# Ticks that end with the query products, and routing placed in the next pass's norm and first recurrence steps

## The chip, the cores and the metric

The kernel runs on one core of one Trainium2 chip. The core has five engines that run their own instruction streams and meet at semaphores: TensorE (PE, matrix products into PSUM; PEld is its weight load), VectorE (DVE), ScalarE (ACT), GpSimd (POOL) and SyncE (SP). Here POOL and SP do no arithmetic: they issue transfers, which all share the core's 16 DMA engines. The metric is the device time of one execution in microseconds (us), lower is better.

## What is computed

A two-layer encoder trunk is applied to two sequences of 256 tokens with 1024 features, in float32. Each layer adds a mixer (a bidirectional state-space recurrence with 8 groups, a dilated attention, a gated merge) and then a feed-forward step whose experts are picked per token:

```python
q = (xt @ w_query).reshape(T, PEER_HEADS, 2, PEER_HALF)
s = jnp.einsum('thsk,snk->thsn', q, sub_keys)
sv, si = lax.top_k(s, PEER_TOPK)                      # 16 of 128, twice per head
cand = sv[:, :, 0, :, None] + sv[:, :, 1, None, :]
cv, ci = lax.top_k(cand, PEER_TOPK)                   # 16 pairs per head
idx = i1 * PEER_N_KEYS + i2
g = jax.nn.softmax(cv, axis=-1)
...
hid = gelu(einsum('td,thkd->thk', xb, expert_u[ib]))
out = einsum('thk,thkd->td', gb * hid, expert_v[ib])
```

With 8 heads and 16 picks a token has 128 expert rows. A row of `expert_u` and the same row of `expert_v` lie side by side in memory, 8 KB together.

## The kernel before

**Passes.** There are four passes (two layers, two sequences each); pass m works on sequence m % 2. A pass has a mixer and 256 ticks. The mixer of pass m runs through the phases `norm`, `ssd` (8 groups), `att` (4 head pairs), `mrg` (8 columns), `out`, `norm2`, `query` (16 products, and after each second one the key scores of a head) and `route`. Its weights come in units of 512 KB, issued by SP into a ring of six slots (L447).

**Ticks.** A tick of pass p is one expert slot for 128 tokens. POOL gathers 128 expert rows of 8 KB, 1 MB in all (L518). DVE multiplies the u half with the normed input and sums it to `hid` (L1374). ACT makes gelu, the weight `wgt` and, where PE is to add the row up, a diagonal matrix `diag` (L993, L997, L1004). Three ticks later the v half is added up, by PE into the PSUM tile `sums` (L810) or by DVE into `x` (L1383); a percentage for each phase says how many of the sums are PE's. There are 8 row buffers `rows`. POOL issues the gather of tick k + 4 at the place of tick k, and that gather first waits for the sum of tick k - 4. When a half is done DVE adds `sums` to `x` (`add_sums`, L1364).

**The order of work.** The ticks of pass m - 1 run during the mixer of pass m. Each engine's program is written out by `together`: the mixer is a generator that yields a place on a planned time line (`EACH` and `TIMES`, the planned us of a phase), and ticks are put in as soon as their due time `DUE` is at or before that place. `TICKS` says how many ticks fall due in each phase and which percentage of sums is PE's. ACT takes each tick 3 planned us late (`BEHIND`). The plan sets the order alone; the engines wait for semaphores. Pass 3's ticks follow after the last mixer with nothing beside them.

**Routing.** `route(m, t, piece)` on DVE turns key scores of 128-token tile t into row numbers in 21 pieces. Pieces 0 to 7 take the best 16 of each head's two score lists, and run in the query phase, both tiles after each other, as soon as ACT has copied that head's scores (`q_sv`). Pieces 8 to 20 are the "late" ones: 8 adds up the candidates, 9 to 12 pick 16 of 112 for two heads each, 13 to 19 turn positions into key numbers, 20 writes `idx` (L1113) and releases the gathers through `i_ok`. `gates` is the softmax's last part, with an Exp on ACT (`softmax`, L832) ahead of it. For tile 0 the late pieces stand in the phase `route` at the end of the pass; for tile 1 they stand in the next pass's first two groups (`LATE_PIECES`).

**Norm.** In `norm` ACT squares x, DVE scales it (L1141), PE transposes it (L563) and DVE writes `hT` (L1147). Then PE makes the step sizes dt (L576), DVE and ACT turn them into decays in a chain of small steps (L1162 to L1181), and PE sums those (`decay_sums`, which waits for `dt_a`). Passes 2 and 3 may square x only once all ticks of the pass two before have been added.

## Time and profile before

| | us |
|---|---|
| median of 3 runs (4110.14 to 4112.36) | 4110.7 |
| the profiled execution, its own time | 4107.11 |
| its span, first to last instruction | 4105.3 |
| PE busy | 3515.4 (86%) |
| DVE busy | 2855.3 (70%) |
| ACT busy | 1838.1 (45%) |
| POOL busy | 1235.4 (30%) |
| moved by DMA | 1444.53 MB, mean 352 GB/s |
| chain that ended last | PE 29%, DMA 29%, DVE 21%, ACT 13%, issue 7% |

The span is the time from the first to the last instruction; a stretch of it is read with the view that gives, for any window, the busy time of each engine, TensorE's granted clock and what the DMA engines moved. The passes can be found in it by the writes of `idx`, which start at 667.0, 1591.9, 2520.3 and 3449.1 us for tile 0.

### The profile page before, as it was taken

To read this page: it belongs to the slowest core of one execution; us is meant where nothing else is said; L and a number is where in the kernel's file an instruction comes from. 1 tells how busy PE (TensorE), PEld (TensorE's weight loads), DVE (VectorE), ACT (ScalarE), POOL (GpSimd) and SP (SyncE) were. 2 spreads that over 40 slices of the span, in tenths; PEclk is the share of its full clock that TensorE was granted. 3 is DMA by queue.
4 is the path that set the end of the run, shared out by engine and by line. 5 is a ranking of instruction groups with operands and counts; after the bars stand their busy time and mean duration, and the time that the engine had idled before them with its cause. 6 is when DMAs were issued, how large, how long until landed. Compare 5 with 4: busy or idle time off the path is not lost.

```text
span 4105.3 us, 41298 instructions
## 1 busy us (share of the span) xinstructions
PE 3515.4 (86%) x13534; PEld 2377.2 (58%) x13534; DVE 2855.3 (70%) x5587; ACT 1838.1 (45%) x4774; POOL 1235.4 (30%) x1094
## 2 busy tenths in 40 slices
PE   7999995998889786989889886989889787778787
PEld 6877874666667564666667664666667663222222
DVE  3631137899877778899877768899787778655454
ACT  4643012676435323676435323676544422343333
POOL 1000001333433322334333322333443223433332
PEclk9999997999999998999999898999999998999999
DMA  6543445999999986999999986999999986999998
GB/s 206 180 153 129 149 136 197 374 418 424 419 412 424 423 336 247 365 423 421 425 416 424 422 335 249 355 424 415 420 423 424 423 341 250 426 427 427 427 427 359
DMA packets 252123, 1444.53 MB, mean 352 GB/s; under 512 B 31608, under 2 KB 31608, under 8 KB 118788
## 3 DMA queue, kind: packets, MB, share of 16 engines
q0 software_dynamic: 164976, 1133.94, 67.4%
q1 hardware_dynamic: 86800, 307.82, 20.2%
q8 instruction: 108, 1.77, 0.2%
q14 instruction: 107, 0.88, 0.1%
q10 hardware_dynamic: 132, 0.12, 0.0%
HBM read 1439.31 MB, written 7.13 MB: 352 GB/s over the span
## 4 chain that ended last, share of the span: by engine, by line
PE 29%; DMA 29%; DVE 21%; ACT 13%; issue 7%; POOL 1%; DVEq 0%; ACTq 0%; POOLq 0%
DMA rows<-in_w_uv,idx 28%; PE banks L551 15%; DVE rows L1374 5%; PE sums L810 5%; DVE x L1383 4%; ACT arena L871 4%; PE banks L766 3%; DVE arena L1191 3%; PE banks L810 2%; ACT diag L1004 1%; ACT L871 1%; ACT L993 1%; PE banks L717 1%; DVE arena L1290 1%; PE banks L687 1%
## 5 line engine op out<-in xcount | busy, mean ns | idle before, releaser
L518 POOL DMA_INDIRECT rows<-in_w_uv,idx x1024 | 1188.0, 1160 | 2198.1 <-DVE x L1383 1114.4
L1374 DVE CUSTOM_DVE_ANT_0 rows<-rows,xn 128x1024 f32<-128x1024 f32 x1024 | 1244.1, 1223 | 568.6 <-DMA rows<-in_w_uv,idx 564.9
L551 PE MATMUL banks<-hT,ring 128*128 128x256 f32 x6656 | 1505.2, 384 | 56.2 <-ACT arena L916 51.5
L551 PEld LDWEIGHTS banks<-hT,ring 128*128 128x128 f32 x6656 | 1277.4, 193 | 320.5 <-issue 85.5
L810 PE MATMUL sums<-rows,diag 128*128 128x512 f32 x1772 | 885.4, 630 | 193.6 <-ACT diag L1004 174.3
L993 ACT ACTIVATE gelu<-hid 128x1 f32<-128x1 f32 x1024 | 205.6, 201 | 1312.4 <-DVE hid L1374 1308.2
L810 PEld LDWEIGHTS sums<-rows,diag 128*128 128x128 f32 x1772 | 333.2, 199 | 600.3 <-ACT diag L1004 302.6
L1383 DVE SCALAR_TENSOR_TENSOR x<-rows,wgt,x 128x1024 f32<-128x1024 f32 x453 | 580.8, 1282 | 0.0
L1191 DVE SCALAR_TENSOR_TENSOR arena<-banks,pr,arena 128x254 f32<-128x254 f32 (+1 forms) x512 | 245.6, 482 | 128.7 <-ACT arena L897 115.0
L997 ACT ACTIVATE wgt<-gelu,gate 128x1 f32<-128x1 f32 x1024 | 302.6, 295 | 33.5
L810 PE MATMUL banks<-rows,diag 128*128 128x512 f32 x512 | 253.9, 618 | 62.0 <-ACT diag L1004 62.0
L1004 ACT ACTIVATE diag<-cst,wgt 128x128 f32<-128x128 f32 x571 | 229.8, 402 | 18.6
L871 ACT ACTIVATE arena<-arena 128x128 f32<-128x128 f32 x768 | 231.6, 393 | 9.4 <-DVE arena L1205 8.8
L551 PE MATMUL banks<-yT,ring 128*128 128x256 f32 x1024 | 226.7, 379 | 0.0
L810 PEld LDWEIGHTS banks<-rows,diag 128*128 128x128 f32 x512 | 86.7, 189 | 229.2 <-ACT diag L1004 167.9
L551 PEld LDWEIGHTS banks<-yT,ring 128*128 128x128 f32 x1024 | 194.6, 190 | 29.0 <-issue 2.9
L993 ACT ACT_TABLE_LOAD x152 | 195.0, 1283 | 2.7
L687 PE MATMUL banks<-ring,hT 128*128 128x384 f32 x512 | 174.1, 493 | 0.0
L766 PE MATMUL banks<-ring,arena 128*128 128x512 f32 x256 | 118.5, 626 | 44.8 <-issue 44.8
L1290 DVE CUSTOM_DVE_ANT_1 arena<-banks,arena 128x768 f32<-128x768 f32 x64 | 60.8, 951 | 111.4 <-PE banks L675 111.4
L687 PEld LDWEIGHTS banks<-ring,hT 128*128 128x128 f32 x512 | 95.8, 191 | 72.1 <-issue 13.1
L717 PE MATMUL banks<-cst,arena 128*128 128x128 f32 x384 | 72.7, 373 | 72.6 <-DVE arena L1302 72.5
(157 smaller groups left out, 2555.2 us busy)
## 6 DMA issues: line engine op xcount, KB each, us to landing
ring<-in_w_ssd SPq DMA_DIRECT2D x192, 512.0 KB
ring<-in_w_att SPq DMA_DIRECT2D x144, 512.0 KB
ring<-in_w_mrg SPq DMA_DIRECT2D x128, 512.0 KB
arena<-a_rows POOLq DMA_DIRECT2D x32, 1024.0 KB
ring<-in_w_qry SPq DMA_DIRECT2D x64, 512.0 KB
arena<-bias_tiles POOLq DMA_DIRECT2D x16, 1152.0 KB
ring<-in_w_out SPq DMA_DIRECT2D x32, 512.0 KB
rows<-in_w_uv,idx POOLq DMA_INDIRECT x1024
```

The lines of the kernel that those rows point to most:

```text
L518: nc.gpsimd.indirect_dma_start(out=rows[n % NB][:, :], out_offset=None, in_=w_uv, in_offset=bass.IndirectOffsetOnAxis(ap=idx[:, t, s:s + 1 ...
L551: mm = pe.matmul(out, w[:, k * P:(k + 1) * P], rhs[:, k0 + k, :], start=start and k == 0, stop=stop and k == n - 1)
L687: mm = pe.matmul(pb(t, 3 * P), hT[:, k, t * P:(t + 1) * P], w[:, k * 3 * P:(k + 1) * 3 * P], start=(k == 0), stop=(k == KD - 1))
L766: mm = pe.matmul(pb(2 * t + nh), mT[:, k, t * P:(t + 1) * P], ring_of(u)[:, nh * 512:(nh + 1) * 512], start=k == 0, stop=k == KD - 1)
L810: mm = pe.matmul(sum_banks(p, t)[:, h, :], diag[e % DIAGS][:, :], rows[n % NB][:, D + 512 * h:D + 512 * h + 512], start=q == mine[0], stop ...
L871: ins = act.activation(Eb[:, r, k, :], Eb[:, r, k, :] if src is None else src, ACT.Exp, bias=bneg[:, si, col:col + 1])
L993: act.activation(gelu[:, k:k + 1], hid[:, k:k + 1], ACT.Gelu).then_inc(g_ge, 1)
L997: act.activation(wgt[:, k:k + 1], gelu[:, k:k + 1], ACT.Copy, scale=gate[:, t, k % SLOTS_T:k % SLOTS_T + 1]).then_inc(g_w, 1)
L1004: act.activation(diag[e % DIAGS][:, :], ident, ACT.Copy, scale=wgt[:, k:k + 1]).then_inc(d_ok, 1)
L1191: ins = v.scalar_tensor_tensor(out=acc, in0=pb(j)[:, lo + o:lo + o + w], scalar=pr[:, col:col + 1], in1=acc, op0=ALU.mult, op1=ALU.add)
L1374: v.tensor_tensor_reduce(u, u, xn2[:, (n // SLOTS_T) % 3, :], 1.0, 0.0, ALU.mult, ALU.add, hid[:, k:k + 1]).then_inc(u_done, 1)
L1383: v.scalar_tensor_tensor(out=xo, in0=rows[before % NB][:, D:], scalar=wgt[:, q:q + 1], in1=xo, op0=ALU.mult, op1=ALU.add).then_inc(v_dve, 1)
```

## The change

Three things are altered together. First, the ticks' table: none falls due in `norm` (6 before) or in `route` (8 before), which is gone as a phase, and the ones of `ssd` begin at 0.55 of group 0. Their count by phase is now 16 up to the end of group 1 (22 before from the start of group 0), 73 in the other groups (72), 76 in `att` (72), 51 in `mrg` (46), 10 in `out` (8), 6 in `norm2` (5) and 24 in `query` (17). The percentage of PE's sums is the same but for the query, 40 (50 before). Second, the late pieces of tile 0 and its `gates` move out of the end of pass m - 1 into pass m's start: piece 8 after the scaling of x, 9 to 12 after `hT`, 13 to 17 after the dt chain, 18 to 20 after the first convolution of group 0, `gates` after the third; the Exp on ACT stands ahead of the second convolution's input there. Third, the late pieces of tile 1 begin one convolution later. After the last mixer, where no pass follows, tile 0's pieces stand by themselves.

```diff
-EACH = {"norm": 20.0, ... "norm2": 14.0, "query": 4.8, "route": 3.0}
+EACH = {"norm": 20.0, ... "norm2": 14.0, "query": 5.4}
...
-TICKS = [("norm", 0, 1, 6, 100), ("ssd", 0, 2, 22, 100), ("ssd", 2, GROUPS, 72, 50), ("att", 0, 4, 72, 20), ("mrg", 0, 8, 46, 15),
-         ("out", 0, 1, 8, 0), ("norm2", 0, 1, 5, 100), ("query", 0, 2 * PH + 1, 17, 50), ("route", 0, REST, 8, 100)]
+TICKS = [("ssd", 0.55, 2, 16, 100), ("ssd", 2, GROUPS, 73, 50), ("att", 0, 4, 76, 20), ("mrg", 0, 8, 51, 15),
+         ("out", 0, 1, 10, 0), ("norm2", 0, 1, 6, 100), ("query", 0, 2 * PH + 1, 24, 40)]
...
-LATE_PIECES = [(0, 1), (2, 3), (4, 5), (6, 7), (8, 9), (10, 11), (12,), ()]
+LATE_PIECES = [(), (0, 1), (2, 3, 4), (5, 6), (7, 8), (9, 10), (11, 12), ()]
...
@@ ScalarE
+                        if m and g == 0 and j == 1:
+                            softmax(m - 1, 0)
                         act.wait_ge(unit.sem, used_up(m, "ssd", g, j))
...
-                yield place("route", REST - 1)
-                softmax(m, 0)
...
             together(mixer, tick, BEHIND)
+            softmax(PASSES - 1, 0)
...
@@ VectorE
+                    if m and w == 0:
+                        route(m - 1, 0, PH)
                     yield place(name, 0, 0.62)
...
                 yield from norm(0, "norm")
+                if m:
+                    for n in range(1, 5):
+                        route(m - 1, 0, PH + n)
                 yield place("norm", 0, 0.92)
...
+                if m:
+                    for n in range(5, 10):
+                        route(m - 1, 0, PH + n)
...
                         conv(g, j)
+                        if m and g == 0 and j == 0:
+                            for n in range(10, REST):
+                                route(m - 1, 0, PH + n)
+                        if m and g == 0 and j == 2:
+                            gates(m - 1, 0)
...
-                for n in range(REST):
-                    yield place("route", n)
-                    route(m, 0, PH + n)
-                yield place("route", REST)
-                gates(m, 0)
...
             together(mixer, tick)
+            for n in range(REST):
+                route(PASSES - 1, 0, PH + n)
+            gates(PASSES - 1, 0)
```

On DVE, at the seam between the mixers of pass 1 and 2, the kernel before has the end of tile 0's routing, the last tick, the adding of the sums, the gates and a tick ahead of the norm (L1112 to L1114 are piece 20, L1364 is `add_sums`, L1121 to L1125 `gates`, L1135 to L1141 the norm):

```order
L1112 TENSOR_SCALAR arena<-arena 128x128
L1113 TENSOR_TENSOR idx<-arena 128x128 [waits k_v]
L1114 TENSOR_TENSOR arena<-arena 128x128
L1374 ISA rows,hid<-rows,xn 128x1024 [waits g_in7]
L1374 ISA hid 128x1
L1364 TENSOR_TENSOR x<-x,sums 128x1024 [waits v_dve,v_pe]
L1121 TENSOR_REDUCE arena<-arena 128x8 [waits s_e]
L1123 RECIPROCAL arena<-arena 128x8 [waits s_v2]
L1125 TENSOR_TENSOR gate<-arena 128x128 [waits s_v2]
L1374 ISA rows,hid<-rows,xn 128x1024 [waits g_in0,xn_ok]
L1374 ISA hid 128x1
L1135 TENSOR_SCALAR stat<-stat 128x2 [waits n_ss]
```

Those of the changed kernel, in the norm that follows the last head's pieces there (its lines are 1 to 15 further down: L1136 to L1142 the norm, L1080 to L1084 piece 8, L1150 `hT`, L1048 the first row of piece 9):

```order
L1136 TENSOR_SCALAR stat<-stat 128x2 [waits n_ss]
L1138 RECIPROCAL stat<-stat 128x2 [waits n_sqrt]
L1142 TENSOR_SCALAR arena<-x,stat 128x1024 [waits par_in,n_rs]
L1142 TENSOR_SCALAR arena<-x,stat 128x1024
L1080 CAST arena<-arena 128x8x2x16 [waits k_v]
L1083 TENSOR_TENSOR arena<-arena 128x8x64
L1084 TENSOR_TENSOR arena<-arena 128x8x48
L1150 TENSOR_TENSOR hT<-banks,pr 128x4x128 [waits n_tr,k_v]
L1150 TENSOR_TENSOR hT<-banks,pr 128x4x128 [waits n_tr] x3
L1048 MAX arena<-arena 128x8
```

No tick is left around the norm, and the routing stands behind the scaling of x instead of ahead of it. Further down on DVE, in group 0 of that pass, the changed kernel writes `idx` between the first convolution (L1201) and the second:

```order
L1201 SCALAR_TENSOR_TENSOR arena<-banks,pr,arena 128x254 [waits c_tap]
L1109 TENSOR_TENSOR arena<-arena 128x2048
L1111 TENSOR_REDUCE arena<-arena 128x128 [waits k_v]
L1113 TENSOR_SCALAR arena<-arena 128x128 [waits k_v]
L1114 TENSOR_TENSOR idx<-arena 128x128 [waits k_v]
L1115 TENSOR_TENSOR arena<-arena 128x128
L1201 SCALAR_TENSOR_TENSOR arena<-banks,pr,arena 128x254 [waits c_acc]
```

So the gathers of the next ticks, which wait for `idx`, are released after the norm, the dt chain and one convolution. On PE the same seam had, before, ten sums (L810, two rows each) between the last key scores (L783) and the transposes (L563), and more between the products that follow. It begins like this (buffer numbers kept):

```order
L783 MATMUL banks<-pr,yT 128x128 [waits q_sv,q_ev]
L783 MATMUL banks<-pr,yT 128x128 x3
L810 MATMUL sums<-rows4,diag0 128x512 [waits d_ok]
L810 MATMUL sums<-rows4,diag0 128x512
L810 MATMUL sums<-rows6,diag1 128x512 [waits d_ok]
L810 MATMUL sums<-rows6,diag1 128x512
```

Of the changed kernel PE has these rows there:

```order
L783 MATMUL banks<-pr,yT 128x128 [waits q_sv,q_ev]
L783 MATMUL banks<-pr,yT 128x128 x3
L810 MATMUL sums<-rows3,diag2 128x512 [waits d_ok]
L810 MATMUL sums<-rows3,diag2 128x512
L810 MATMUL sums<-rows6,diag3 128x512 [waits d_ok]
L810 MATMUL sums<-rows6,diag3 128x512
L563 MATMUL banks<-cst,arena 128x128 [waits n_xn,q_sv,q_ev]
L563 MATMUL banks<-cst,arena 128x128 x7
L563 MATMUL banks<-cst,arena 128x128 [waits n_xn]
L563 MATMUL banks<-cst,arena 128x128 x7
L576 MATMUL banks<-pr,hT 128x64 [waits par_in,hT_ok]
```

Two of the ten sums are left there, and the next one comes after group 0's sixth product.

## Rows read from the trace of the kernel before

**Rows 1.** The page's 40 slices: what the DMA engines moved in each, in GB/s.
```profile
GB/s 206 180 153 129 149 136 197 374 418 424 419 412 424 423 336 247 365 423 421 425 416 424 422 335 249 355 424 415 420 423 424 423 341 250 426 427 427 427 427 359
```
**Rows 2.** Windows: length, busy PE, PEld, DVE, ACT, POOL (instructions), PEclk, DMA share, GB/s.
```profile
637.20:667.00 29.80, 0.01 (x1) 0.00 (x0) 29.00 (x118) 1.88 (x2) 0.00 (x0) 0.56 0.04 15
...
738.00:1401.00 663.00, 597.07 (x2495) 438.56 (x2496) 545.89 (x811) 378.98 (x952) 246.69 (x207) 0.96 1.01 416
1401.00:1471.80 70.80, 44.57 (x112) 22.72 (x111) 52.11 (x71) 19.95 (x54) 23.33 (x19) 0.76 0.97 393
1471.80:1550.40 78.60, 78.13 (x358) 62.56 (x357) 57.85 (x263) 19.70 (x61) 20.15 (x16) 1.00 0.86 322
1550.40:1592.00 41.60, 20.18 (x34) 6.87 (x32) 41.15 (x134) 8.51 (x25) 5.58 (x5) 0.79 0.45 164
1592.00:1668.50 76.50, 63.85 (x240) 41.72 (x240) 55.63 (x158) 35.78 (x82) 26.18 (x24) 0.89 0.82 306
1668.50:1728.00 59.50, 58.31 (x223) 39.93 (x224) 46.04 (x73) 47.30 (x118) 17.45 (x16) 1.00 0.97 380
```
**Rows 3.** A window of the last ticks, gathers alone: length, busy POOL (gathers), PEclk, DMA, GB/s.
```profile
3500.00:4000.00 500.00, 198.91 (x202) 0.99 1.01 427
```
**Rows 4.** POOL in order of time: start, length, issue, idle before and what ended it.
```profile
1573.62 1.08 POOL L518 DMA_INDIRECT rows<-in_w_uv,idx  x1 [7.81 <-DVE x L1383]
1592.46 1.88 POOL L518 DMA_INDIRECT rows<-in_w_uv,idx  x1 [17.75 <-DVE idx L1113]
```
**Rows 5.** DVE in order of time, the query phase of the second pass.
```profile
1487.30 0.29 DVE L1047 MAX8 arena<-arena 128x8 f32<-128x128 f32 x1 [13.11 <-ACT arena L974]
...
1491.98 1.22 DVE L1374 CUSTOM_DVE_ANT_0 rows<-rows,xn 128x1024 f32<-128x1024 f32 x1
...
1493.11 1.30 DVE L1383 SCALAR_TENSOR_TENSOR x<-rows,wgt,x 128x1024 f32<-128x1024 f32 x1
1494.31 1.23 DVE L1374 CUSTOM_DVE_ANT_0 rows<-rows,xn 128x1024 f32<-128x1024 f32 x1
...
1496.82 0.29 DVE L1047 MAX8 arena<-arena 128x8 f32<-128x128 f32 x1 [1.27 <-ACT arena L974]
```
**Rows 6.** DVE in order of time, tile 0's late pieces of pass 0.
```profile
642.69 0.29 DVE L1079 CAST arena<-arena 128x256 bf16<-128x256 uint32 x1
...
652.90 0.23 DVE L1092 TENSOR_SCALAR arena<-arena 128x128 uint32<-128x128 uint32 x1
...
663.11 1.23 DVE L1108 TENSOR_TENSOR arena<-arena 128x2048 bf16<-128x2048 bf16 x1
...
666.95 0.29 DVE L1113 TENSOR_TENSOR idx<-arena 128x128 uint32<-128x128 f32 x1
```
**Rows 7.** DVE in order of time, the norm, the dt chain and the first convolution behind.
```profile
674.35 0.16 DVE L1135 TENSOR_SCALAR stat<-stat 128x2 f32<-128x2 f32 x1
674.78 0.17 DVE L1137 RECIPROCAL stat<-stat 128x2 f32<-128x2 f32 x1 [0.27 <-ACT stat L849]
674.98 1.42 DVE L1141 TENSOR_SCALAR arena<-x,stat 128x1024 f32<-128x1024 f32 x2
...
691.18 0.29 DVE L1162 TENSOR_TENSOR arena<-banks,pr 128x128 f32<-128x128 f32 x1 [4.66 <-PE banks L576]
...
695.79 0.22 DVE L1181 TENSOR_SCALAR arena<-arena 128x128 f32<-128x128 f32 x1
...
699.98 2.04 DVE L1191 SCALAR_TENSOR_TENSOR arena<-banks,pr,arena 128x254 f32<-128x254 f32 x4 [0.53 <-ACT arena L897]
```
**Rows 8.** PE in order of time: kernel start, then pass 1's norm after a pause.
```profile
21.71 7.09 PE L576 MATMUL banks<-pr,hT 128*128 128x64 f32 x32 [0.78 <-DVE hT L1147]
28.58 12.97 PE L551 MATMUL banks<-hT,ring 128*128 128x256 f32 x48
...
675.89 3.65 PE L563 MATMUL banks<-cst,arena 128*128 128x128 f32 x16 [38.68 <-DVE arena L1141]
...
687.46 3.68 PE L576 MATMUL banks<-pr,hT 128*128 128x64 f32 x32
```
**Rows 9.** End of group 0: a tick on ACT, and PE's first product of group 1.
```profile
1661.62 0.20 ACT L993 ACTIVATE gelu<-hid 128x1 f32<-128x1 f32 x1 [0.18 <-DVE hid L1374]
...
1668.54 3.72 PE L551 MATMUL banks<-hT,ring 128*128 128x256 f32 x16 [0.57 <-ACT arena L916]
```

4 lines of the change are left out of this document (2 added, 2 removed).

## The prediction

> **What bounds the kernel now.** I read the page's slices first. From the eighth on the DMA engines move 412 to 427 GB/s nearly everywhere; the exceptions are one or two slices at each of three seams, with 247 GB/s in the deepest, and the tail [rows 1]. A window of 500 us in the last ticks moves 427 GB/s with 202 gathers, 2.46 us each (1.0486 MB by 427 GB/s) [rows 3]. So the kernel is bound by DMA, and its time is the bytes, which the change leaves alone, by that rate, plus whatever time DMA stands idle. The windows by stage show where it does. Groups 1 to 7, attention and merge run at 416 GB/s for 663 us: nothing is free there. `out` and `norm2` have 393, the query 322 with PE busy 78.13 of 78.60 us, the routing 164 with DVE busy 41.15 of 41.60, and the norm with group 0 306 [rows 2]. The query of pass 1 starts at 1471.8, group 1 of pass 2 at 1668.5: 196.7 us in which DMA is idle for 19 + 26 + 22 = 67, each window's length by its share of 427 GB/s that is missing. These seams are what the change rebuilds. The order, which the change writes by hand, tells what follows what; the durations below are rows.
>
> **The seam after the change, as a chain on DVE.** First the query. It holds 24 ticks instead of 17. The first head's pieces start 15.5 us after the query's start, and still do. One head's pieces for both tiles take 4.68 us (1487.30 to 1491.98), a tick 1.14, a sum on DVE 1.2; today DVE then idles 1.27 us for ACT's copy of the next scores, since PE sets the pace at 9.5 us a head (1487.30 to 1496.82) [rows 5]. Between the first and the last head's pieces now stand 20 ticks, 14 DVE sums and one adding of sums (about 1.15), beside seven heads' pieces: 22.8 + 16.8 + 1.2 + 32.8 = 73.6 us. DVE becomes the slowest there, by little: PE has 16 x 3.45 + 8 x 0.9 + 11 sums x 1.72 = 81 us from the query's start, DVE 15.5 + 73.6 + 4.7 = 93.8 until the last head's pieces are done. I call that point R. In passes 1 to 3 it is the query's start + 93.8; in pass 0, without ticks, it stays at 642.7 [rows 6].
>
> From R on: square root and reciprocal 0.6, the scaling 1.4 with piece 8 (1.4) behind it; `hT` waits for PE's transposes (0.9 after the scaling's start, 3.65 long) and ends at R + 5.8 [rows 6 to 8]. Pieces 9 to 12 take 8.8 (piece 8 ends at 644.1; 652.90), the dt chain 4.8 (691.18 to 696.0), pieces 13 to 17 10.2 (652.90 to 663.11), a convolution 2.0, pieces 18 to 20 up to `idx` 4.1 [rows 6, 7]. So `idx` comes at R + 35.7. Of the pauses that were to take the routing, the first is 0.27 us and the one for PE's dt products 4.66 [rows 7]; 24.5 us of pieces don't fit into them, so most of the routing is on this chain, and the overlap is PE's: dt products and six units run beside it. Then 0.9 for the Exp and ACT's input to the second convolution, three convolutions 6.0, gates and the two small copies 1.4, two ticks 2.3, and tile 1's pieces 8 to 14, which the table puts into group 0: 1.4 + 8.8 + 4.3 = 14.5. After the second tick's product (today at 1661.5) come silu, gelu and the copy on ACT, 7.0 us until PE's first product of group 1 (1668.54) [rows 9]. From `idx` that is 32.1, together R + 68.
>
> **What the seams give.** Pass 0 to 1: group 1 starts at 642.7 + 68 = 710.7 against 738.0 (the windows cut there): -27. Passes 1 to 2 and 2 to 3: 93.8 + 68 = 161.8 against 196.7 (1471.8 to 1668.5) [rows 2]: -35 each. After pass 3 no norm follows: `idx` at R + 24.3 (642.69 to 666.95), so query's start + 118.1, against 120.1 today (3449.1 for a query from 3329.0): -2, and -1 more because the gathers behind the first four need not wait for the old sums. In all -100.
>
> **What it costs.** Between the start of group 1 and the next query there were 11 + 72 + 72 + 46 + 8 + 5 = 214 ticks; now 12 + 73 + 76 + 51 + 10 + 6 = 228. These 14 gathers a pass have no idle DMA to fall into but a bit in group 1 (380 GB/s) and in `out` and `norm2` (393) [rows 2]: 14 x 2.46 = 34.4, less 3 for that slack, so +31 for a pass, +94 for three.
>
> **TensorE's clock.** PE now idles some 20 us at the end of group 0, waiting for DVE, and between the last key scores and the transposes. Rows show both levels: with granted clock 0.56 in the pause ahead (1.2 GHz is 0.5 of full speed) [rows 2], the 16 transposes at 675.89 took 3.65 us; the dt products took 7.09 at kernel start and 3.68 at 687.46, and three units 12.97 against 10.4 [rows 8]. So a restart after a pause costs up to 3.4 + 2.5 = 6 us of PE. At the norm DVE's chain hides it (dt done at R + 13 even so, wanted at R + 14.6). In group 1 PE is busy 58.31 of 59.50 us [rows 2], and there it shows: between 0 and 6 for each of three seams; I take 2, since DVE and DMA are close behind, +6. The Trainium skill, "TensorE: Matmul & The Clock Gate", section "What's actually happening", says that the throttled clock is the default and that activity releases it. The rows agree. By that rule alone each restart would pay in full, and the sum would be 12 us higher.
>
> **The sum.** -100 + 94 + 6 = 0. The profiled execution took 4107.1 us (span 4105.3 and 1.8 around it), 3.6 under the median of 4110.7; the difference of 0 goes to the median: 4111. What the change really does is to move DMA's idle time: in the seam DMA waits from the last gather (after the change some 15 us before R, as the last four ticks and R's pieces follow it) to `idx` at R + 36, about 50 us against 19 today (1573.62 to 1592.46) [rows 4], and in exchange has fewer bubbles around it.
>
> **Rivals.**
> *Faster: the added ticks are cheap.* The 14 ticks a pass would fall into DMA bubbles. For: from group 1 to the next query about 20 of 734 us are still idle (663 us at 416 and 71 at 393, of 427), and denser ticks could close half. Against: those bubbles are where buffers are full, in group 1. Price: 9 us less a pass, 27 in all: 4084.
> *Slower: the query falls into step.* DVE's route pieces wait for ACT's copy of scores behind PE's products; PE waits for diagonals of ticks that DVE has just done. If the 1.27 us idle of each head [rows 5] stays although DVE is now the slowest, the query grows by 8 x 1.27 = 10 us a pass in three passes: 4141. It decides as soon as PE's sums stand less than a head behind DVE. Against: sums lag three ticks.
> *Slower: the clock.* At full price, and again after each short wait in group 0, 6 to 8 us a seam instead of 2: +12 to +18, 4126.
> *It doesn't do what it says.* The pauses take little of the routing; if ACT's or PE's answers also came late at each of the handoffs (Exp, second convolution's input, dt), 2 to 3 us each, `idx` and group 1 come 8 us later, three times: 4135. With rows of 0.27 to 0.54 for such answers [rows 7] I find it unlikely.
>
> **How the numbers follow.** About 0.2% (8 us) is what a measurement can tell from no change. The forecast, a balance within some 20 us, has 0.52; the cheap ticks 0.22; the query in step 0.12; the clock 0.08; the late answers 0.06. The forecast's own spread comes from two sums of some 100 us that cancel, each good to a tenth: a third of it lies beyond 8 us below, less than that above. Faster: 0.22 + 0.13 = 0.35. Slower: 0.26 with the bulk of its three rivals, plus some of the forecast's, in all 0.28. The rest, 0.37, is no change. The range reaches from the cheap ticks, 4085, to between the clock and the query in step, 4137.
>
> **What would show it.** `idx` of tile 0 at about 678, 36 us after the last head's pieces in passes 1 and 2, and group 1's first product 68 us after them; if these differ, the chain is wrong. From group 1 to the next query about 765 us instead of 734 (663 + 71); if it is 755 or less, the added ticks were cheap. DVE without the 1.27 us waits in the query, and that phase near 94 us to the last head's pieces. In the slices, deeper but narrower dips. The granted clock near 0.5 in group 0's end, and three units slower than 10.4 us behind it. It would be wrong above all if the 14 ticks were priced wrongly, as each 0.2 us of their price is 8 us of the sum.

## The result, and the profile after the change

| | before | after |
|---|---|---|
| median, us | 4110.4 (4103.4 to 4112.4, 8 runs) | 4121.3 (4118.4 to 4125.9, 8 runs) |
| the profiled execution, its own time | 4107.1 | 4118.9 |
| its span | 4105.3 | 4116.8 |
| DVE busy | 2855.3 | 2913.3 |
| PE busy | 3515.4 | 3462.0 |

The changed kernel takes 1.0029 times as long, 95% interval 1.0018 to 1.0040: a little slower, 10.9 us by the medians, where no change was forecast (4111, range 4085 to 4137).

The page's slices answer to [rows 1]. The dips at the seams are deeper and narrower, as the prediction said (204, 198 and 210 GB/s in one slice each, where before it was 247 to 250 with a second slice at 335 to 341):

```profile
GB/s 196 169 163 128 148 140 141 397 419 412 409 414 419 423 401 204 373 417 413 414 414 418 424 402 198 374 416 414 410 419 420 423 399 210 427 427 427 427 427 358
```

The windows by stage answer to [rows 2], with the same columns. In order: pass 0's last pieces up to `idx`; groups 1 to 7, attention and merge, which end 19 us later than before and are cut 4.8 us ahead of the last product of merge, as in [rows 2]; `out` and `norm2`; the query of pass 1; from there to `idx`; the rest of group 0; the first 59 us of group 1.

```profile
641.10:681.60 40.50, 32.87 (x164) 29.22 (x165) 38.68 (x142) 8.48 (x14) 0.00 (x0) 0.83 0.23 73
715.60:1420.10 704.50, 612.11 (x2517) 444.21 (x2518) 574.71 (x847) 387.04 (x981) 254.53 (x219) 0.94 1.01 413
1420.10:1484.10 64.00, 46.26 (x105) 21.90 (x105) 54.02 (x72) 17.32 (x53) 27.25 (x21) 0.79 1.01 422
1484.10:1564.60 80.50, 80.03 (x362) 63.33 (x361) 69.30 (x276) 22.28 (x73) 23.68 (x20) 1.00 0.97 385
1564.60:1614.60 50.00, 38.17 (x162) 30.91 (x161) 48.18 (x153) 11.54 (x22) 0.00 (x0) 0.76 0.20 63
1614.60:1646.80 32.20, 9.11 (x28) 5.68 (x26) 30.74 (x111) 10.56 (x23) 11.60 (x11) 0.63 0.83 314
1646.80:1706.00 59.20, 58.16 (x218) 39.05 (x219) 42.77 (x67) 45.33 (x111) 15.81 (x16) 1.00 0.93 346
```

The query moves 385 GB/s where it moved 322, and `out` with `norm2` 422 where it was 393, in 64.0 us instead of 70.8 and with three ticks more: those took up ticks. From the query's end to `idx` DMA is nearly still (63 GB/s). The seam from the query's start to group 1's first product is 1646.8 - 1484.1 = 162.7 us, where it was 196.7. The stretch from there to the next query (1646.8 to 2412.4) is 765.6 us, where it was 731.7 (1668.5 to 2400.2).

**The ledger of the two profiled executions.** Each line is the time between two marks in the trace, after less before.

| stretch | after less before | the prediction's term |
|---|---|---|
| pass 0, up to its last key scores | +3.9 | 0 |
| from there to group 1 of pass 1 | -26.3 | -27 |
| the two other seams, query's start to group 1 | -34.0, -33.9 | -35, -35 |
| group 1 to the next query, three times | +34.7, +33.9, +33.6 | +31 and +2 each |
| after pass 3's query | -0.4 | -3 |
| sum | +11.5 | 0 |

One execution is not the kernel's usual time. The same kernel once more (e0_again below) was profiled in an execution of 4111.5 us, 7 under its median. There pass 0 gave +2.4, the first seam -25.1, the two others -34.0 and -34.1, the three long stretches +33.8, +30.9 and +30.1, the end +0.1, together +4.1. So the seams are sure to about 1 us, and the long stretches are not: they cost 34.1 on the mean in one execution and 31.6 in the other.

The chain on DVE in the seam after pass 1, in order of time (start, length, the engine's line, what it writes, and in brackets the idle time before). These rows answer to [rows 5] to [rows 7]: the last head's pieces, the norm's first step, `hT`, the end of the routing, the second convolution, group 0's mask, group 1's first convolution.

```profile
1574.75 0.28 DVE L1048 MAX8 arena<-arena 128x8 f32<-128x128 f32 x1
...
1579.43 0.15 DVE L1136 TENSOR_SCALAR stat<-stat 128x2 f32<-128x2 f32 x1
...
1582.77 2.56 DVE L1150 TENSOR_TENSOR hT<-banks,pr 128x512 f32<-128x512 f32 x4
...
1614.64 0.29 DVE L1114 TENSOR_TENSOR idx<-arena 128x128 uint32<-128x128 f32 x1
...
1615.96 2.04 DVE L1201 SCALAR_TENSOR_TENSOR arena<-banks,pr,arena 128x254 f32<-128x254 f32 x4 [0.83 <-ACT arena L899]
...
1642.08 2.35 DVE L1215 TENSOR_TENSOR arena<-arena,cst 128x1024 f32<-128x1024 f32 x2
...
1655.78 2.04 DVE L1201 SCALAR_TENSOR_TENSOR arena<-banks,pr,arena 128x254 f32<-128x254 f32 x4 [7.91 <-ACT arena L899]
```

The last head's pieces end at 1579.43, which is the query's start + 95.3 (93.8 forecast); `idx` comes 35.2 us later (35.7), and group 1's first product 67.4 us later (68).

PE in the same place answers to [rows 8] and [rows 9] (L633 and L639 are the last products of group 0):

```profile
1580.95 3.65 PE L563 MATMUL banks<-cst,arena 128*128 128x128 f32 x16 [7.94 <-DVE arena L1142]
1585.38 7.09 PE L576 MATMUL banks<-pr,hT 128*128 128x64 f32 x32 [0.78 <-DVE hT L1150]
1592.26 12.92 PE L551 MATMUL banks<-hT,ring 128*128 128x256 f32 x48
...
1607.39 10.63 PE L551 MATMUL banks<-hT,ring 128*128 128x256 f32 x48
...
1639.87 3.75 PE L810 MATMUL sums<-rows,diag 128*128 128x512 f32 x4 [21.84 <-ACT diag L1004]
1643.41 1.71 PE L633 MATMUL banks<-arena 128*128 128x256 f32 x4
1644.96 0.60 PE L639 MATMUL banks<-cst,arena 128*128 128x128 f32 x4
1646.81 3.72 PE L551 MATMUL banks<-hT,ring 128*128 128x256 f32 x16 [1.26 <-ACT arena L918]
1650.37 1.88 PE L810 MATMUL sums<-rows,diag 128*128 128x512 f32 x4
```

The dt products (7.09 us against 3.68 [rows 8]) and the first three units (12.92 us, the next three 10.63) run at the slow clock, 1.2 GHz, and are hidden by DVE's pieces: DVE waits for none of them. PE pauses 21.84 us at the end of group 0, and the next four summing products take 3.75 us, at the slow clock (1.88 for four of them at 1650.37). L639 takes 0.60, as it does elsewhere at the full clock, and the first products of group 1 take 3.72, the same as before [rows 9].

POOL in order of time answers to [rows 4]. The last gather of pass 1 is issued at 1557.02, the first of the next at 1615.20. Three follow at once, and the fifth stands behind the write of the decay rows (L485), which waits 11.52 us for DVE's copies; L479 then reads them back:

```profile
1557.02 1.68 POOL L518 DMA_INDIRECT rows<-in_w_uv,idx  x1 [5.24 <-DVE x L1393]
1615.20 0.94 POOL L518 DMA_INDIRECT rows<-in_w_uv,idx  x1 [56.51 <-DVE idx L1114]
...
1631.59 0.58 POOL L485 DMA_DIRECT2D a_rows<-arena  x1 [11.52 <-DVE arena L1275]
1632.48 0.98 POOL L518 DMA_INDIRECT rows<-in_w_uv,idx  x1 [0.30 <-issue]
1633.85 0.75 POOL L479 DMA_DIRECT2D arena<-a_rows  x1 [0.39 <-DMA a_rows<-arena]
```

### The profile page after: what moved, and what is told of

Same layout as the page of the kernel before. It is cut to its first block, busy times and chain, and to the rows that moved or that the text cites. A ratio compares the mean times of both kernels' runs of the same rounds, so it can differ in the third digit from the quotient of the medians.

```text
span 4116.8 us, 40895 instructions
## 1 busy us (share of the span) xinstructions
PE 3462.0 (84%) x13342; PEld 2354.7 (57%) x13342; DVE 2913.3 (71%) x5635; ACT 1794.7 (44%) x4714; POOL 1225.1 (30%) x1094
## 4 chain that ended last, share of the span: by engine, by line
PE 30%; DMA 26%; DVE 23%; ACT 13%; issue 6%; POOL 1%; DVEq 0%; ACTq 0%
DMA rows<-in_w_uv,idx 25%; PE banks L551 14%; DVE rows L1384 5%; DVE x L1393 5%; PE sums L810 5%; ACT arena L871 4%; PE banks L810 3%; PE banks L766 3%; DVE arena L1201 3%; PE banks L687 2%; ACT diag L1004 2%; ACT L871 1%; PE banks L608 1%; ACT L993 1%; DVE arena L1227 1%
## 5 line engine op out<-in xcount | busy, mean ns | idle before, releaser
L810 PE MATMUL sums<-rows,diag 128*128 128x512 f32 x1580 | 807.9, 640 | 285.5 <-ACT diag L1004 253.5
L810 PEld LDWEIGHTS sums<-rows,diag 128*128 128x128 f32 x1580 | 301.8, 202 | 650.0 <-issue 327.8
L1393 DVE SCALAR_TENSOR_TENSOR x<-rows,wgt,x 128x1024 f32<-128x1024 f32 x501 | 641.6, 1281 | 10.0 <-ACT wgt L997 9.4
L1201 DVE SCALAR_TENSOR_TENSOR arena<-banks,pr,arena 128x254 f32<-128x254 f32 (+1 forms) x512 | 245.3, 481 | 156.4 <-ACT arena L899 142.6
L810 PE MATMUL banks<-rows,diag 128*128 128x512 f32 x512 | 253.9, 618 | 62.2 <-ACT diag L1004 62.2
L810 PEld LDWEIGHTS banks<-rows,diag 128*128 128x128 f32 x512 | 86.7, 189 | 229.4 <-ACT diag L1004 168.2
L1004 ACT ACTIVATE diag<-cst,wgt 128x128 f32<-128x128 f32 x523 | 210.0, 401 | 17.1
L608 PE MATMUL banks<-arena 128*64 128x256 f32 x512 | 91.0, 518 | 83.4 <-DVE arena L1227 83.4
```

The costliest lines, as they stand in the source:

```text
L810: mm = pe.matmul(sum_banks(p, t)[:, h, :], diag[e % DIAGS][:, :], rows[n % NB][:, D + 512 * h:D + 512 * h + 512], start=q == mine[0], stop ...
L1004: act.activation(diag[e % DIAGS][:, :], ident, ACT.Copy, scale=wgt[:, k:k + 1]).then_inc(d_ok, 1)
L1201: ins = v.scalar_tensor_tensor(out=acc, in0=pb(j)[:, lo + o:lo + o + w], scalar=pr[:, col:col + 1], in1=acc, op0=ALU.mult, op1=ALU.add)
L1393: v.scalar_tensor_tensor(out=xo, in0=rows[before % NB][:, D:], scalar=wgt[:, q:q + 1], in1=xo, op0=ALU.mult, op1=ALU.add).then_inc(v_dve, 1)
```

## The experiments

All ratios are to the kernel before, from runs on the same chip. For most of them I cut a pass into two parts at marks that hold in every version: the **seam**, from the query's start to the sums that begin `weigh` in group 1 (L1222; the late pieces of both tiles all lie in it), and the **rest**, from there to the next query's start. The windows below are those two parts between passes 1 and 2, columns as in [rows 2]. DMA's idle time in a part is its length times the share of 427 GB/s that is missing. Before, then after:

```profile
1471.80:1700.70 228.90, 194.33 (x750) 134.24 (x749) 180.88 (x595) 88.22 (x226) 61.58 (x53) 0.93 0.79 299
1700.70:2400.20 699.50, 610.06 (x2485) 438.86 (x2485) 571.89 (x841) 375.00 (x946) 258.60 (x217) 0.94 1.00 415
```

```profile
1484.10:1680.60 196.50, 161.09 (x674) 123.69 (x673) 173.08 (x575) 68.57 (x177) 44.05 (x40) 0.88 0.74 284
1680.60:2412.40 731.80, 627.10 (x2497) 443.10 (x2496) 598.72 (x875) 380.23 (x975) 272.43 (x230) 0.92 1.01 414
```

POOL's count in brackets is nearly the number of gathers: 53 and 217 before, 40 and 230 after. Thirteen ticks went from the seam to the rest; the seam lost 32.4 us and the rest gained 32.3, which is 2.5 us for each of the 13.

| run | median, us | ratio (95%) | seam | rest |
|---|---|---|---|---|
| before | 4110 | 1 | 228.9 | 699.5 |
| after | 4121.3 | 1.0029 (1.0018 to 1.0040) | 196.5 | 731.8 |
| e0_again, after once more | 4118.6 | 1.0029 (1.0019 to 1.0040) | 196.5 | 728.8 |
| e1_place | 4151.2 | 1.0104 (1.0089 to 1.0120) | 205.4 | 729.7 |
| e2_end | 4104.1 | 0.9984 (0.9975 to 0.9993) | 224.0 | 700.8 |
| e3_late | 4136.5 | 1.0064 (1.0051 to 1.0078) | 200.5 | 737.8 |
| e4_early | 4079.9 | 0.9931 (0.9917 to 0.9945) | 201.2 | 713.9 |
| e5_even | 4106.2 | 0.9995 (0.9986 to 1.0004) | 196.5 | 725.2 |
| e6_bytes | 4028.6 | 0.9808 (0.9794 to 0.9821) | 196.5 | 715.2 |
| e7_decay | 4061.2 | 0.9886 (0.9871 to 0.9901) | 195.8 | 722.7 |
| e8_copies | 4074.8 | 0.9921 (0.9908 to 0.9935) | 201.7 | 713.1 |
| e9_more | 4058.1 | 0.9881 (0.9865 to 0.9896) | 202.3 | 709.3 |
| e10_share | 4111.9 | 1.0003 (0.9994 to 1.0012) | 196.5 | 728.8 |
| e11_dense | 4115.1 | 1.0012 (1.0003 to 1.0022) | 196.5 | 729.0 |

The seam repeats to 0.1 us from one profiled execution to the next. The rest does not: 731.8 and 728.8 for the same kernel, and in e7_decay 717.5, 722.7 and 716.1 in the three passes. What is said of it below leans on the mean of the three and on the medians. Three profiled executions lie far from the median of their kernel: e0_again's 7 us below, e6_bytes's 8 and e7_decay's 10 above.

### Placement alone, and the query's ticks alone

**e1_place** keeps the table and tile 1's list of the changed kernel and puts tile 0's pieces, gates and softmax back where they were:

```diff
-                    if m and w == 0:
-                        route(m - 1, 0, PH)
...
+                for n in range(REST):
+                    yield place("route", n)
+                    route(m, 0, PH + n)
+                yield place("route", REST)
+                gates(m, 0)
```

> The changed kernel with its table of ticks and its list of late pieces, but tile 0's pieces, gates and softmax are back at the end of the pass, ahead of the next norm. The pauses of the norm are then empty and the pieces take their time one after the other. Theory A (the pauses hide work): pieces 8 to 12 ran in the changed kernel beside the transposes (7.9 us of VectorE idle in the trace of before with four ticks in it) and 13 to 20 mostly beside the wait for dt; empty pauses are about 12 us, so group 1's first product comes at the last head's pieces + 79 instead of + 67.4, idx about 7 us earlier (+ 28 instead of + 35); three seams at 12 us more: 4121 + 36 = 4157 us. Theory B (the seam is shorter only because 14 ticks left it, the filling is worth nothing): 4121 us, with the product at + 67.

Measured: 4151.2 us.

```profile
1499.90:1705.30 205.40, 156.16 (x674) 119.30 (x673) 175.00 (x575) 68.77 (x177) 44.93 (x40) 0.88 0.71 273
1705.30:2435.00 729.70, 623.97 (x2497) 443.15 (x2496) 598.86 (x875) 380.12 (x975) 268.37 (x230) 0.93 1.01 415
```

The seam is 8.9 us longer with the same ticks in it (x40 both times), and DVE's pauses in the norm are back, the longest being this one:

```profile
1633.84 0.29 DVE L1162 TENSOR_TENSOR arena<-banks,pr 128x128 f32<-128x128 f32 x1 [3.88 <-PE banks L576]
```

With the waits for ACT and PE at the gates, the norm and `hT` they add to 9.2 us. So theory A holds, B falls: filling the pauses is worth 9 us a seam (12 forecast; the first seam, 16 us, is more than this accounts for), and the other 24 of the 32.4 us are the 13 ticks that left, some 1.8 us each. This is the whole of the balance: the 13 ticks save 24 us in the seam and cost 32 in the rest, and the filled pauses give 9.

**e2_end** takes the other half alone: the kernel before, with 24 ticks in the query (planned 5.4 us a product there, as in the change) and none among tile 0's pieces.

```diff
-         ("out", 0, 1, 8, 0), ("norm2", 0, 1, 5, 100), ("query", 0, 2 * PH + 1, 17, 50), ("route", 0, REST, 8, 100)]
+         ("out", 0, 1, 8, 0), ("norm2", 0, 1, 6, 100), ("query", 0, 2 * PH + 1, 24, 40)]
```

> The kernel before, with one thing of the change alone: the last 8 ticks of a pass, which ran between tile 0's pieces, run in the query stage (24 there instead of 17) and in norm2 (6 instead of 5). The 14 ticks in the norm and group 0 stay in the seam, and the placement of the pieces is the kernel's before. Theory A (a gather costs nothing more where the query stage has idle DMA time, and each tick costs 1.15 us of VectorE in the seam and some waits): the query stage about 1.8 us longer as in the changed kernel, from its end to group 1's product 118 - 8 - 6 (the wait of 7.8 us for the last sums goes mostly) = about 110 to 104; per seam -4 to -8, total 4110 - 18 = 4092 us (4085 to 4100). Theory B' (the query stage pays 2.46 us for each tick put into it): 7 x 2.46 x 4 = 69 us less 3 x 12 = 4143 us.

Measured: 4104.1 us.

```profile
1477.30:1701.30 224.00, 176.07 (x722) 127.73 (x721) 186.89 (x597) 82.76 (x216) 60.21 (x53) 0.89 0.78 305
1701.30:2402.10 700.80, 612.44 (x2489) 440.58 (x2489) 573.47 (x843) 375.04 (x949) 261.08 (x218) 0.94 1.00 415
```

A gain of 4.9 us a seam, at the lower end of what was expected (4 to 8), and 1.3 lost in the rest; the whole gained 7 us where 18 were expected, so the time lies outside the 4085 to 4100 of theory A. B' (each of the seven ticks paid in full in the query) falls by much more. So this part of the change is good by itself, if small: the loss comes from the 14 ticks that left the norm and group 0.

### What ends the seam

**e3_late** takes tile 1's late pieces out of group 0, where seven stood ahead of or about the mask, and puts four of them into the pause of 7.91 us ahead of group 1's first convolution:

```diff
-LATE_PIECES = [(), (0, 1), (2, 3, 4), (5, 6), (7, 8), (9, 10), (11, 12), ()]
+LATE_PIECES = [(), (), (), (), (4, 5), (6, 7), (8, 9, 10), (11, 12)]
...
                         yield place("ssd", g, 0.07)
+                        if m and g == 1:
+                            for n in range(4):
+                                route(m - 1, 1, PH + n)
```

> The changed kernel, but tile 1's late pieces leave group 0: pieces 8 to 11 stand ahead of group 1's first convolution, where VectorE waited 7.9 us, and the others behind group 1's convolutions two or three at a time. Theory A (VectorE's work in the seam is what sets group 1's start, and DMA idle time there is total time): seven pieces of 2.1 us leave, group 1's first product comes 10 to 14 us earlier after the last head's pieces (about + 55 instead of + 67.4); group 1 pays 3 pieces, up to 6 us; per seam -4 to -12, total 4121 - 28 = 4093 us (4085 to 4109). Theory C (the time of the seam is given back in full by a group 1 that is then bound by VectorE): 4121 us.

Measured: 4136.5 us, slower by 15 than the changed kernel. Group 1's first product did come 12 us earlier in the seam (1637.07 - 1486.40 = 150.7 us after the query's start instead of 162.7), as expected. DVE and PE in order of time show what became of it:

```profile
1642.21 2.36 DVE L1215 TENSOR_TENSOR arena<-arena,cst 128x1024 f32<-128x1024 f32 x2 [6.41 <-DMA arena<-a_rows]
...
1686.85 1.22 DVE L1222 TENSOR_TENSOR arena<-arena 128x1024 f32<-128x1024 f32 x1
```

```profile
1637.07 3.72 PE L551 MATMUL banks<-hT,ring 128*128 128x256 f32 x16 [0.92 <-ACT arena L918]
...
1690.52 1.98 PE L608 MATMUL banks<-arena 128*64 128x256 f32 x8 [10.81 <-DVE arena L1227]
```

With the pieces gone, DVE waits 6.41 us for the decay rows ahead of the mask, and behind it has all 13 pieces to do before `weigh`; PE runs ahead and then waits 10.81 us for it. All late pieces stand ahead of `weigh(0)` in DVE's order, since they work in memory that the first group's results (`y3`) take right behind it, so group 1's first product was the wrong mark. The seam ends where DVE's chain does, at `weigh`, and that came 4.0 us later (200.5). The rest got longer too, 737.8, at 406 GB/s:

```profile
1486.40:1686.90 200.50, 166.81 (x681) 125.83 (x679) 174.26 (x576) 69.39 (x179) 46.25 (x42) 0.89 0.76 298
1686.90:2424.70 737.80, 625.83 (x2488) 444.11 (x2489) 599.34 (x876) 380.34 (x973) 269.53 (x229) 0.92 0.99 406
```

Theory A is wrong in its first half, and C's case (given back in full) is what happened, and more.

### What a tick costs in the rest

**e4_early** brings four ticks of the rest back into group 0:

```diff
-TICKS = [("ssd", 0.55, 2, 16, 100), ("ssd", 2, GROUPS, 73, 50), ("att", 0, 4, 76, 20), ("mrg", 0, 8, 51, 15),
+TICKS = [("ssd", 0.36, 0.6, 4, 100), ("ssd", 0.6, 2, 16, 100), ("ssd", 2, GROUPS, 72, 50), ("att", 0, 4, 74, 20), ("mrg", 0, 8, 50, 15),
...
-                        if m and g == 0 and j == 2:
+                        if m and g == 0 and j == 1:
                             gates(m - 1, 0)
```

> The changed kernel, but gates of tile 0 stand behind group 0's second convolution instead of its third, and four ticks of a pass stand between there and the fourth convolution; group 2 to 7, attention and merge have 1, 2 and 1 ticks fewer. Theory A (a tick in the stages that move 410 to 420 GB/s costs its gather, 2.46 us, and one in the seam 1.15 us of VectorE): per pass -9.8 + 4.6 = -5.2, three passes: 4121 - 16 = 4105 us, with group 1's product about 4.6 us later and the stages from there to the query about 9.8 us shorter. Theory D (a tick is cheaper in the full stages than a gather, about 1 us): 4121 us or 4 us more.

Measured: 4079.9 us, 41 under the changed kernel.

```profile
1464.10:1665.30 201.20, 170.04 (x686) 127.54 (x685) 179.06 (x583) 72.17 (x190) 55.43 (x45) 0.89 0.77 296
1665.30:2379.20 713.90, 618.70 (x2497) 440.17 (x2496) 590.53 (x863) 377.88 (x965) 268.88 (x227) 0.95 1.01 419
```

The seam paid 4.7 us, four times DVE's 1.15, as theory A has it. But the rest gained 17.9 (16.5 on the mean of three passes, 13.8 against e0_again), not 9.8: its DMA idle time fell, from 731.8 x 13/427 = 22 us to 713.9 x 8/427 = 13. So the changed kernel had lost more there than the gathers' own time.

**e5_even** asks where, with one number:

```diff
-TICKS = [("ssd", 0.55, 2, 16, 100), ("ssd", 2, GROUPS, 73, 50), ("att", 0, 4, 76, 20), ("mrg", 0, 8, 51, 15),
+TICKS = [("ssd", 0.55, 2, 16, 100), ("ssd", 2, GROUPS, 72, 50), ("att", 0, 4, 76, 20), ("mrg", 0, 8, 52, 15),
```

> The changed kernel with one number moved: groups 2 to 7 have 72 ticks (12 in each, as before) instead of 73, and merge 52 instead of 51. Nothing else moves. In the changed kernel the stretch from group 2's to attention's start lasts 241 to 244 us with 73 ticks, where the run with four early ticks lasts 235.0 to 235.5 with 72. Theory E (a count that does not divide by six breaks the step of groups, ticks and buffers, and leaves DMA idle time beyond the tick's 2.46 us): these groups get 6 to 8 us shorter, merge 2.5 longer, -4 to -5 a pass, three passes: 4107 us. Theory F (the extra is the price of any tick above the 216 of that run, wherever it stands): no change, 4121 us.

Measured: 4106.2 us, 12 to 15 under the changed kernel. Groups 2 to 7, then attention and merge, pass 2. The changed kernel:

```profile
1690.90:1934.80 243.90, 223.50 (x875) 155.85 (x873) 213.61 (x327) 173.85 (x447) 91.36 (x79) 0.94 1.01 409
1934.80:2359.50 424.70, 352.91 (x1496) 262.72 (x1493) 329.94 (x479) 184.62 (x470) 156.91 (x134) 0.91 1.01 417
```

e5_even:

```profile
1686.80:1921.60 234.80, 218.53 (x875) 154.12 (x873) 210.65 (x322) 171.30 (x443) 88.95 (x77) 0.98 1.01 416
1921.60:2349.50 427.90, 352.51 (x1495) 264.61 (x1494) 333.44 (x482) 186.96 (x474) 155.38 (x136) 0.92 1.01 421
```

The groups lose 9.1 us, attention and merge gain 3.2. In the two other passes the groups take 238.8 and 237.8, against 241.4 and 243.9, so 2.6 and 6.1 less. Theory E holds: the 73rd tick costs about 6 us on the mean, in place of 2.5. All other runs agree: on the mean of three passes these groups take 242.5 to 243.9 us in the five kernels with 73 ticks and 235.7 to 237.2 in the eight with 72.

**e11_dense** tells an uneven count from a high one: 13 ticks in each group, fewer in attention and merge.

```diff
-TICKS = [("ssd", 0.55, 2, 16, 100), ("ssd", 2, GROUPS, 73, 50), ("att", 0, 4, 76, 20), ("mrg", 0, 8, 51, 15),
+TICKS = [("ssd", 0.55, 2, 16, 100), ("ssd", 2, GROUPS, 78, 50), ("att", 0, 4, 73, 20), ("mrg", 0, 8, 49, 15),
```

> The changed kernel with 13 ticks in each of groups 2 to 7 (78 instead of 73), 73 in attention (76) and 49 in merge (51); the sum is the same. e5_even, with 12 in each group and 76 and 52, took 4106 us, its groups 2 to 7 about 235 to 239 us. Theory E (a group count that divides evenly keeps the step; only 73 broke it): groups 2 to 7 take 235 + 6 x 2.46 = 250 us, attention and merge 6 ticks less, 4106 us as e5_even. Theory N (it is density: the 13th tick of a group finds the buffers or an engine behind, and costs the 6 to 8 us that the 73rd tick cost, in every group): 235 + 6 x 7 = 277 us, less 15 in attention and merge, some 27 us a pass more: 4187 us; with other work that gives way in part, at least 4130.

```profile
1689.50:1940.60 251.10, 225.03 (x886) 156.38 (x884) 220.32 (x335) 175.67 (x458) 100.09 (x83) 0.97 1.01 415
```

The groups take 251.1 us, and 250.0 and 250.4 in the other passes, six times 2.46 over 235, as theory E has it. Density is no trouble there; 73 was. But the whole came to 4115.1, between e5_even and the changed kernel. The 73 and 49 of attention and merge, which divide evenly into neither four head pairs nor eight chunks, are not the reason: from the end of the groups to the next query it takes 468 us on the mean for 138 ticks, where e4_early (74 and 50) takes 469 for 140 and e5_even (76 and 52) 480 for 144. In the profiled executions the rest is only 1.1 us longer than e5_even's; where the other microseconds of the medians lie was not found.

**e6_bytes** takes 14 MB a pass away and leaves the ticks; it leaves out the expert rows of 14 ticks, which are computed from old rows:

```diff
+                if k in range(100, 212, 8):
+                    pool.dma_start(rows[n % NB][:, 0:64], w_uv[0:P, 0:64]).then_inc(g_in[n % NB], 16)
+                    return
                 nc.gpsimd.indirect_dma_start(
```

> The changed kernel, but 14 gathers of each pass (every eighth from slot 100 to 204, in attention and merge) fetch 32 KB by a plain transfer instead of 1 MB of expert rows; the rest of their ticks (VectorE's product and sum, TensorE's sums, ScalarE's gates) stays. So 14 of 256 experts of a token are computed from old rows. Theory A (from group 1's end to the query, and in the tail, the time is the bytes' time): 14 x 2.46 = 34 us in each of four passes, 4121 - 137 = 3984 us, and group 1's end to the next query 698 instead of 732. Theory G (VectorE, which is busy 0.90 to 0.92 of that stretch, or the order of the work, is as near a bound): less than half of that, above 4053 us.

Measured: 4028.6 us, 90 under the changed kernel on the same chip. It fell between the two theories. From the last query's start to the end, the changed kernel and this one:

```profile
3340.90:4116.80 775.90, 593.74 (x1393) 241.73 (x1391) 455.80 (x1014) 269.05 (x868) 278.54 (x278) 0.96 0.92 386
```

```profile
3292.00:4034.20 742.20, 583.23 (x1393) 245.00 (x1391) 453.79 (x1014) 269.02 (x868) 279.79 (x278) 0.96 0.92 384
```

There the whole 34 us are gained: the tail is bound by bytes. In the rest beside a mixer it is 16.6 of 34.4 (13.7 on the mean of three passes against e0_again):

```profile
1662.30:2377.50 715.20, 618.08 (x2497) 439.45 (x2496) 597.10 (x876) 380.33 (x975) 271.52 (x230) 0.93 0.99 404
```

DMA's idle time grows there from 22 to 38 us. So at this number of ticks the bytes are the bound by only some 15 us a pass; behind them stands the ticks' own work with the mixer's. (The share of 0.90 to 0.92 that the expectation gives for VectorE there is too high: it is 0.82, 598.72 of 731.8 us.) The prediction's sentence that the time is the bytes' time plus idle is an identity; it does not say that the idle part stays when the bytes change.

**e10_share** asks whether that second bound is DVE, by moving sums from it to PE.

```diff
-TICKS = [("ssd", 0.55, 2, 16, 100), ("ssd", 2, GROUPS, 72, 50), ("att", 0, 4, 76, 20), ("mrg", 0, 8, 52, 15),
+TICKS = [("ssd", 0.55, 2, 16, 100), ("ssd", 2, GROUPS, 72, 50), ("att", 0, 4, 76, 35), ("mrg", 0, 8, 52, 30),
```

> e5_even (12 ticks a group) with the share of sums on TensorE raised in attention from 20 to 35 in a hundred and in merge from 15 to 30: some 19 sums a pass of 1.3 us leave VectorE and become 1.8 us of TensorE and a diagonal on ScalarE. The run with 14 small gathers gained only 16 of 34 us a pass there, so something other than bytes is near. Theory L (that is VectorE, busy 0.8 of attention and merge, behind whose sums GpSimd's next gather waits most often): the idle DMA time there goes down by 3 to 5 us a pass, 4106 - 12 = 4094 us. Theory M (TensorE's queue is as near, its waits for the diagonals grow): 4106 us or some us more.

Measured: 4111.9 us, ratio 1.0003 against e5_even's 0.9995. In the rest DVE's busy time fell by 22 us and PE's rose by 26, and the stretch did not get shorter. Theory L falls. Which chain is the second bound stays open.

### Two steps further

**e7_decay** builds on e4_early: `bneg` and `aT` ahead of the late pieces, and three of these in the pause at group 1's start.

```diff
-LATE_PIECES = [(), (0, 1), (2, 3, 4), (5, 6), (7, 8), (9, 10), (11, 12), ()]
+LATE_PIECES = [(), (0, 1), (2, 3), (4,), (8, 9), (10, 11), (12,), ()]
...
+                        if m and g == 1:
+                            for n in (5, 6, 7):
+                                route(m - 1, 1, PH + n)
...
+                        if g == 0 and j == 2:
...
                         if m and g < 2:
                             for n in LATE_PIECES[4 * g + j]:
```

> The kernel of the run with four early ticks, with VectorE's order in group 0 changed once more: the two copies that release the decay rows (bneg and aT) stand ahead of the late pieces behind the third convolution, not behind them, and three of tile 1's pieces move from group 0 to the pause ahead of group 1's first convolution (4.4 us there). In that run GpSimd's sixth gather waits for these copies and group 0's mask for the decay rows. Theory H (from idx on the seam is set by how early GpSimd gets past the decay rows, and by VectorE's chain up to group 1's sums): the copies 5 to 6 us earlier, 4 to 8 us less a seam, 4080 - 18 = 4062 us. Theory I (from idx on the DMA engines are full anyway, the seam can't get shorter): 4080 us.

**e8_copies** has the order of the two copies alone, and after's list of late pieces:

```diff
-                        if m and g < 2:
-                            for n in LATE_PIECES[4 * g + j]:
-                                route(m - 1, 1, PH + n)
                         if g == 0 and j == 2:
...
+                        if m and g < 2:
+                            for n in LATE_PIECES[4 * g + j]:
+                                route(m - 1, 1, PH + n)
```

> The run with four early ticks, with one of the two edits of the run e7_decay alone: the two copies that release the decay rows stand ahead of the late pieces behind group 0's third convolution. (e7_decay also moved three late pieces into the pause ahead of group 1's first convolution; it took 4061 against 4080 us.) Theory H1 (what counts is how early GpSimd gets past the decay rows, since from idx on the seam goes at the pace of the gathers): most of the 18 us, 4062 to 4068 us. Theory H2 (what counts is VectorE's chain to group 1's sums, shortened by the pieces that fill a pause; the order of the copies alone leaves that chain as long): 4076 to 4080 us.

Measured: 4061.2 us for both edits, 4074.8 for the copies alone, beside 4079.9 for e4_early, from which the copies alone can't be told apart (0.9908 to 0.9935 against 0.9917 to 0.9945). In e7_decay the seam is 5.4 us shorter than in e4_early:

```profile
1463.60:1659.40 195.80, 168.61 (x678) 126.49 (x677) 177.48 (x582) 71.96 (x189) 49.83 (x44) 0.89 0.78 300
```

POOL in e8_copies shows why the copies alone do so little. Its write of the decay rows is issued at 1606.82, 143.4 us after the query's start, where it was 149.3 in e4_early (1613.42); but it is only 5 us behind six gathers (issued from 1594.56 on), where in e4_early it is 11 us behind them, and the read that follows it waits 6.41 us, so that the read comes only 1.6 us earlier. e4_early, then e8_copies:

```profile
1613.42 0.58 POOL L485 DMA_DIRECT2D a_rows<-arena  x1 [10.50 <-DVE arena L1275]
...
1618.64 0.75 POOL L479 DMA_DIRECT2D arena<-a_rows  x1
```


```profile
1606.82 0.58 POOL L485 DMA_DIRECT2D a_rows<-arena  x1 [4.61 <-DVE arena L1272]
...
1616.33 0.74 POOL L479 DMA_DIRECT2D arena<-a_rows  x1 [6.41 <-DMA a_rows<-arena]
```

The mask then starts at 1627.22, which is 163.8 us after the query's start, and so it does in e4_early. The seam is 201.7. So e7_decay's time, which theory H had forecast (4062), has another reason. H2 is the better account: the three pieces in the pause (2.0, 2.3 and 1.2 us, together 5.5) shorten DVE's chain up to `weigh`, which is the 5.4. The copies have a part in it even so. With two pieces fewer ahead of it, e7_decay's mask starts 161.1 us after the query's start, and it waits for the decay rows there, which in e4_early come 163.8 us after it:

```profile
1624.66 2.36 DVE L1215 TENSOR_TENSOR arena<-arena,cst 128x1024 f32<-128x1024 f32 x2 [1.59 <-DMA arena<-a_rows]
```

The pieces without the copies were not run.

**e9_more** is e7_decay with four more ticks out of attention and merge.

```diff
-TICKS = [("ssd", 0.36, 0.6, 4, 100), ("ssd", 0.6, 2, 16, 100), ("ssd", 2, GROUPS, 72, 50), ("att", 0, 4, 74, 20), ("mrg", 0, 8, 50, 15),
-         ("out", 0, 1, 10, 0), ("norm2", 0, 1, 6, 100), ("query", 0, 2 * PH + 1, 24, 40)]
+TICKS = [("ssd", 0.36, 0.6, 4, 100), ("ssd", 0.6, 2, 18, 100), ("ssd", 2, GROUPS, 72, 50), ("att", 0, 4, 72, 20), ("mrg", 0, 8, 48, 15),
+         ("out", 0, 1, 10, 0), ("norm2", 0, 1, 6, 100), ("query", 0, 2 * PH + 1, 26, 40)]
```

> e7_decay with four more ticks of a pass out of attention (74 to 72) and merge (50 to 48): two into groups 0 and 1 (16 to 18), two into the query stage (24 to 26). The DMA engines have some 5 us idle from idx to group 1's end in e7_decay and 7.6 in the query. Theory A (the ticks go where DMA time is idle): 4 x 2.46 = 10 us less in attention and merge, 2 x 1.15 more in the seam, 2 to 4 more in the query: -4 to -6 a pass, 4061 - 15 = 4046 us. Theory K (the seam from idx on and VectorE in the query are full, so each tick costs there what it saves): 4061 us.

Measured: 4058.1 us, ratio 0.9881 against 0.9886. The rest is 10 us shorter on the mean of three passes, the seam 6.5 longer and the end 3: theory K, nearly even. This and e7_decay are the fastest here, 1.1 to 1.2% under the kernel before.

### The changed kernel once more

> The changed kernel once more, unaltered. In its profiled execution pass 0, whose instructions are the same as before, ended its key scores 3.9 us later than in the profiled execution of before (641.1 against 637.2). Theory A: that is chance of single executions, between 638 and 642 in any of these kernels, and the median is 4121 us again, of which the ledger of the seams explains 7 to 8 us over before. Theory J: the change itself delays pass 0; 641 again.

Measured: 4118.6 us, the same ratio. Its profiled execution has pass 0's last key scores at 639.6, and the other versions, whose pass 0 is the same, between 637.1 (e5_even) and 641.1 (e7_decay). So the +3.9 in the ledger is for the most part chance: theory A. The medians are 11 to 12 us over before all the same, so the kernel's usual time holds some 4 us that this ledger, without the +3.9, does not place.

## Why the prediction was right, and where it was off

**The chain on DVE in the seam** was right to a few tenths: `idx` 35.2 us after the last head's pieces (35.7 worked out), group 1's product 67.4 (68). The point from which these count, the query's start + 93.8, came at 95.3. The seams gave 26.3, 34.0 and 33.9 (27, 35 and 35).

**Two parts, told apart.** The time was forecast rightly, but the forecast of the seam did not say how much of it was the filling of pauses and how much the ticks that leave. e1_place does: 9 and 24. It also spoke of a first pause of 0.27 us and one of 4.66; the pauses that were filled add to 9.2, as the norm's handoffs to ACT and PE come to the same amount again.

**The end of pass 3** gave 0.4 instead of 3. That term was mis-sized: the query is 1.5 us longer than worked out, and the gathers behind the first four gained nothing that shows. The gathers' own pause in a seam was sized too short as well, without harm to the sum: the last one is issued 22 us ahead of the end of the last head's pieces and the next 58 us after it (1557.02 to 1615.20), where 15 and about 50 were said.

**What it cost.** 14 gathers at 2.46 us are 34.4; measured 34.7, 33.9 and 33.6 in one execution, 33.8, 30.9 and 30.1 in the other. The term of +31 was right for the gathers and lacked one thing. The slack was there: `out` and `norm2` went from 393 to 422 GB/s, which is 5 us of idle time used. But in groups 2 to 7, 73 ticks instead of 72 cost 6 us on the mean instead of 2.5. The medians show what that is worth: with 72 and 52 (e5_even) the kernel takes 4106.2, 12 to 15 us less, or 4 to 5 a pass, and its stretch from group 1 to the next query is 762.9 us on the mean of three passes, 30.4 over before, which is the forecast's +31. This price is more than the whole distance between the forecast and the measured time. The rows of before could not show this price; the table's number could have been held against the six groups.

**TensorE's clock.** +2 a seam was assumed, in group 1. The granted clock did fall, to 0.63 on the mean of group 0's rest, and the sum and L633 there ran slow (3.75 and 1.71 us), but the first product of group 1 took 3.72, and from 1646.8 on the granted clock is 1.00. Group 1's products up to L639 take 44.1 us (1646.8 to 1690.9) against 42.5 (1668.5 to 1711.0), with one tick more in them; that leaves next to nothing for the clock. The 3.65 us of the transposes, which the prediction read as a slow row, are no sign of it: they take 3.3 to 3.7 us in all norms of both kernels, and no row shows what the slow clock adds to them. The Trainium skill, "TensorE: Matmul & The Clock Gate", section "What's actually happening", has the throttled clock as the default that activity releases. The trace agrees: after the pause the sum and L633 run slow and L639, right behind them, runs at full speed, so the clock was back before it counted. By the rule alone, each restart in full, the sum was 12 us higher and would have been nearer to the time, for the wrong reason.

**The rivals.** *The added ticks are cheap* (4084): no, 2.4 to 2.5 us each in one execution, 2.2 to 2.4 in the other. Yet e6_bytes shows that half of a gather's price there is not the transfer's. *The query in step* (4141): no. DVE's waits of 1.27 us for ACT's copy are all but gone, the query moves 385 GB/s, and its last pieces are 1.5 us late, not 10. *The clock at full price* (4126) comes nearest in time and is refuted by the row of 3.72. *Late answers* (4135): the handoffs cost 0.27 and 0.83 us; no.

**The sum.** Off by 11. In the one profiled execution 5.3 us of it are seams and end, 2.2 the cost, 3.9 pass 0, which is mostly chance in single executions. That the cost missed by so little there is partly luck: the 3.5 us a pass that the 73rd tick cost beyond its gather have against them the 2 a seam of the clock, which did not come. The forecast of no change for a balance of two terms near 100 was right in kind; the sign of what was left hung on 5% of either. It had asked for that much care: each 0.2 us of a tick's price is 8 us of the sum.

**A mark that was wrong without harm.** The prediction let the seam end at group 1's first product. For the change itself this made no difference, since DVE's chain moved as a whole. e3_late shows that the mark doesn't bear a step further: what ends the seam is DVE's chain up to `weigh(0)`.

## What to carry to other kernels

When work is moved out of a stretch where one engine sets the pace into one where transfers do, each piece changes its price, here from 1.2 (e4_early) to 1.8 us (e1_place) in the seam to some 2.5 us in the rest: move as few as the order allows, and bring back those that can stand as early as their input. Count against the loop, and try the neighbours of a number: over six groups 72 and 78 cost 2.5 us a piece, and the one that made 73 more than twice that. That the remainder as such is the reason is not shown: 73 is the only such number tried there, and in merge, where 46, 49, 50, 51 and 52 ticks over eight chunks all leave one, no surcharge is seen: from attention to the next query the versions go from 454 us for 131 ticks to 480 for 144, about 2 us for each. And before a stage's end is taken as a mark, look for the last reader of what the moved work produces or occupies; shifting work past the first mark that looks like the end gains nothing when the same engine owes it before the second.

## What the runs showed of the hardware

A small transfer issued close behind large ones waits for them: the write of the decay rows landed 2.0 us after its issue in the changed kernel, where the last of four gathers had been issued 11.5 us earlier, 9.2 us in e8_copies, 4.6 us behind six, and 10.8 us in e3_late, 1.6 us behind four. In e4_early, 10.5 us behind six, the read was not held up by it at all: the 5.2 us between the two (1613.42 to 1618.64) are POOL's issue of two gathers. Issuing the write 6 us earlier in the seam, in e8_copies, brought the read forward by 1.6 us and the mask by nothing.

A count of 73 goes with a somewhat lower granted clock in groups 2 to 7: 0.94 to 0.97 in the passes of the five kernels with 73 ticks, 0.96 to 0.99 in those of the eight with 72, 0.97 to 0.98 with 78. Whether that is a cause of the lost time or a consequence of PE's waits was not told apart.

Taking 14 gathers of 1 MB out of a pass gave back the whole transfer time in the tail (34 us) and less than half of it beside the mixer (13.7 to 16.6 us). DMA's busy share beside the mixer was 1.01 with them and 0.99 without: the busy share does not show by how much the transfers are the bound.
